# First branch of a hybrid layer: each direction's weights applied apart, with the tokens on the partitions

## The chip, the core and the metric

One NeuronCore of a Trainium2 chip runs the whole program. The metric is the device time of one execution in microseconds, the lower the better. The engines are TensorE (PE; PEld are its weight loads), VectorE (DVE), ScalarE (ACT), GpSimd (POOL), and SyncE (SP), which only issues transfers here.

## What is computed

Two "hybrid" layers (context of 256 and latent of 256 tokens, 1,024 channels) are followed by a second block of two layers. All of it is fp32. The change lies in the hybrid layers' first branch, a gated linear attention (mLSTM) with 4 heads (query and key 128 wide, value 256), run over the tokens forwards and backwards:

```
a   = exp(dmat - m_row) * (q k^T)            # per direction; dmat masks keys behind or ahead
den = sum_s(a)
h   = (a @ v) / max(|den|, exp(-m_row))      # per direction
y_a = rmsnorm(h_fwd + h_bwd) * a_norm_w * sigmoid(o) * silu(z)      # norm over a head's 256 channels
y   = sigmoid(mg_a) * (y_a @ w_a_out) + sigmoid(mg_b) * ... + sigmoid(mg_c) * ...
```

The reference does this in chunks with a carried state. The kernel computes the masked 512 x 512 weights of each head in closed form. In layer 1 only the 256 latent tokens are queries; keys and values are all 512.

## The kernel before

Each engine runs a program written out by hand, one Python function per engine (`tensor_program`, `scalar_program`, `vector_program`, `pool_program`, `sync_program`), and each of them calls `branch_a(l)`, `merge(l, "a")`, `branch_b(l)` and so on, in this order. The order of the work is the order of the calls. Between engines a `wait_ge` waits for a named event of another engine (`("a_av", l, h, c)` is the value product of layer l, head h, half c). Nothing is planned at run time.

**Weights.** `plan_units` lists the weight matrices in units of 2,048 words per partition, in the order of use. SyncE loads a unit into one of two `raw` buffers. `convert(u)` splits it: ScalarE rounds it to fp32r (`wh`, L1306 and L1307), VectorE subtracts to get the rest (`wl`, L1837 and L1839). `used(tag, j)` stands in both programs where a unit has been used up, and converts the unit two further on. A projection is three fp32r matmuls per 128 input channels (`mm3`, through `mm` at L483): `proj_t` gives channels on the partitions, tokens in the columns; `proj_k` gives tokens on the partitions (the values).

**The head loop of the first branch.** Everything of a token lies in four tiles of 128; layer 1 uses tiles 2 and 3 as queries. In TensorE's `branch_a`, for head h:

1. "pick": two 4-row matmuls broadcast the head's row of log weights to banks 2 and 3. ScalarE's exponentials and VectorE's `a_diag` (with the masks) turn it into `a_f` and `a_b`, one [key, query] matrix per direction.
2. Scores: four matmuls into banks 4 to 7, keys on the partitions, queries in the columns. VectorE multiplies them into `a_f` and `a_b` (`a_at`).
3. Projections o and z (banks 0 and 1, two halves each); ScalarE applies sigmoid and silu.
4. Denominators: `a_f` and `a_b` times a column of ones (one-column matmuls into bank 2); VectorE forms the reciprocal in four small operations; eight matmuls spread it over all partitions (`a_rd`).
5. VectorE multiplies the spread reciprocals into `a_f` and `a_b`; GpSimd adds the two (`a_mix`). TensorE meanwhile projects q and k of head h + 1.
6. Value product (`a_av`): value stationary, mixed weights moving, output channels on the partitions, into banks 4 and 5. It waits for GpSimd.
7. Between the two halves of the value projection of head h + 1, the sums of squares over the 256 channels are taken by one-column matmuls (`sums`); VectorE's `root` finds the inverse square root in 12 small operations; after the second half, `spread` broadcasts it, ScalarE copies it out (`a_rr`), VectorE multiplies it in (`a_y`), and GpSimd applies the gate.
8. ScalarE writes the rounded result to `YB[0]`, GpSimd the rest to `YB[1]`: the merge's operand.

The next head's pick waits for `a_mix`, its scores for `a_y` and `a_rr`. After head 3 there are no projections of a next head; steps 4 to 7 run alone, and then `merge` starts with two gate projections. The matmuls of steps 2, 4, 6 and 7 are plain fp32 and show as two records each. The two memsets of `a_f` and `a_b`, once a layer, and the products in steps 5, 7 and 8 are GpSimd's `branch_a`.

A helper records each operation, so one line stands for many: L483 is any matmul, L487 any transpose, L1296 any activation, L1818, L1822, L1823, L1826 and L1829 are VectorE's `tt`, `ts`, `stt` and `cp`, L2547 is GpSimd's `tt`. Groups are told apart by their tiles: TM is the scratch area that holds all `a_` tiles, colS the small columns, PS the PSUM banks, T the constant tables.

Of the kernel before, what the change touches and what calls it, by code (L numbers as in the profile page):

```python
# [198 lines left out]
def program(nc, wpk, xin, memt, vec, tabs, tabs2, rpb, out):  # L199
# [10 lines left out]
    with ctx:  # L210
# [123 lines left out]
        def lay(l):  # L334
# [11 lines left out]
        a_fg = [a_hs[p, 0] for p in dirs]  # L346
        a_zero = [a_hs[p, 1] for p in dirs]
# [7 lines left out]
                   {0: ((256, 512),), 1: ((0, 128), (256, 512)), 2: (), 3: ((256, 384),)})  # L355

# [122 lines left out]
        def tensor_program(P):  # L479
# [53 lines left out]
            def ada_unit(q):  # L533
# [48 lines left out]
            def branch_a(l):  # L582
# [2354 lines left out]
```

## Time and profile before

| | |
|---|---|
| median of 3 runs | 2703.24 us (2700.78 to 2704.4) |
| the profiled execution | 2704.5 us, its span 2702.7 us |
| TensorE busy | 2452.9 us (91%), 16,496 records |
| VectorE busy | 1322.9 us (49%) |
| ScalarE busy | 1030.7 us (38%) |
| GpSimd busy | 335.9 us (12%) |
| transfers | 291.48 MB, mean 108 GB/s |

The span is the stretch from the first to the last instruction, and the execution's time has a little around it. A busy TensorE isn't one at its peak, since the ends of matmuls are modelled: the distance between the starts of two of them is the better measure. Its clock is granted at one of two levels, 1.2 and 2.4 GHz; PEclk in a stretch is the mean as a share of the upper one.

### The profile page before, as it was taken

How to read it: one execution, taken by the hardware profiler on the slowest of the kernel's cores; microseconds unless marked ns; L12 is line 12 of the kernel's file. 1: busy time of each engine (PE TensorE's matmuls, PEld its weight loads, DVE VectorE, ACT ScalarE, POOL GpSimd, SP SyncE). 2: the span in 40 equal slices, each digit the busy share in tenths (PEclk: the TensorE clock that was granted, in tenths of full speed). 3: DMA queues.
4: the chain of work that ended last, by engine and by line, in shares of the span. 5: the costliest groups of instructions: out<-in, count | busy, mean ns of one | idle time of the engine just before them, and what ended most of it. 6: DMA issues, size and time to landing. Idle time of an engine off the chain costs nothing.

```text
span 2702.7 us, 38973 instructions
## 1 busy us (share of the span) xinstructions
PE 2452.9 (91%) x16496; PEld 2196.6 (81%) x16496; DVE 1322.9 (49%) x2682; ACT 1030.7 (38%) x1893; POOL 335.9 (12%) x340
## 2 busy tenths in 40 slices
PE   6999989999988999779889999997898999888998
PEld 3777767988867988668889888897767999867998
DVE  4433322577633223553345665345655555656554
ACT  2333311344431222243333444444354444444443
POOL 1011110222201021011112230110100010100010
PEclk9899989999999999889889999998898999988999
DMA  5211114211123212132223223444213445302444
GB/s 231 94 55 55 63 63 167 99 63 63 56 101 140 94 52 104 55 99 77 78 94 141 79 79 125 141 173 141 94 63 109 163 171 191 130 19 105 172 168 144
DMA packets 50413, 291.48 MB, mean 108 GB/s; under 512 B 8960, under 2 KB 13312, under 8 KB 19072
## 3 DMA queue, kind: packets, MB, share of 16 engines
q1 hardware_dynamic: 50240, 289.00, 30.1%
q8 instruction: 129, 2.11, 0.3%
q14 instruction: 44, 0.36, 0.0%
HBM read 286.89 MB, written 2.36 MB: 107 GB/s over the span
## 4 chain that ended last, share of the span: by engine, by line
PE 72%; DVE 14%; ACT 5%; DMA 3%; issue 1%; SPq 1%; POOL 1%; DVEq 0%; ACTq 0%; POOLq 0%
PE PS L483 70%; DVE wl L1837 3%; DMA raw<-in_wpk 3%; ACT wh L1306 2%; DVE wl L1839 2%; PE PS L487 2%; DVE TM L1818 1%; ACT TM L1296 1%; ACT TMG L1296 1%; DVE colS L1826 1%; DVE HYl L1826 1%; DVE TMG L1826 1%; POOL TM L2547 1%; ACT HYh L1296 1%; DVE TM L1826 1%
## 5 line engine op out<-in xcount | busy, mean ns | idle before, releaser
L483 PE MATMUL PS<-HYh,wh 128*128 128x256 f32 (+1 forms) x3000 | 966.2, 322 | 58.2 <-DVE HYl L1826 30.5
L483 PE MATMUL PS<-HYl,wh 128*128 128x256 f32 (+1 forms) x3000 | 948.8, 316 | 0.0
L483 PE MATMUL PS<-HYh,wl 128*128 128x256 f32 (+1 forms) x3000 | 948.0, 316 | 0.0
L1837 DVE TENSOR_TENSOR wl<-raw,wh 128x1280 fp32r<-128x1280 f32 (+2 forms) x254 | 368.6, 1451 | 720.8 <-ACT wh L1306 720.8
L483 PEld LDWEIGHTS PS<-HYh,wh 128*128 128x128 f32 x3000 | 590.9, 197 | 105.1 <-DVE HYl L1826 35.5
L483 PEld LDWEIGHTS PS<-HYl,wh 128*128 128x128 f32 x3000 | 591.0, 197 | 29.5
L483 PEld LDWEIGHTS PS<-HYh,wl 128*128 128x128 f32 x3000 | 589.0, 196 | 31.7
L1306 ACT ACTIVATE wh<-raw 128x1280 fp32r<-128x1280 f32 (+2 forms) x254 | 306.6, 1207 | 386.0 <-PE PS L483 246.8
L1296 ACT ACTIVATE TM<-PS 128x512 f32<-128x512 f32 (+4 forms) x363 | 175.4, 497 | 720.0 <-PE PS L483 590.6
L483 PE MATMUL PS<-wh,HYh 128*128 128x256 f32 x1458 | 424.5, 291 | 13.0 <-DVE HYl L1826 11.2
L483 PE MATMUL PS<-wl,HYh 128*128 128x256 f32 x1458 | 414.5, 284 | 0.0
L483 PE MATMUL PS<-wh,HYl 128*128 128x256 f32 x1458 | 414.5, 284 | 0.0
L483 PEld LDWEIGHTS PS<-wh,HYh 128*128 128x128 f32 x1458 | 281.4, 193 | 17.9 <-DVE HYl L1826 12.0
L483 PEld LDWEIGHTS PS<-wl,HYh 128*128 128x128 f32 x1458 | 281.4, 193 | 0.3
L483 PEld LDWEIGHTS PS<-wh,HYl 128*128 128x128 f32 x1458 | 281.2, 193 | 0.1
L483 PE MATMUL PS<-TM 128*128 128x128 f32 (+5 forms) x848 | 215.1, 440 | 60.8 <-DVE TM L1826 22.7
L1839 DVE TENSOR_TENSOR wl<-raw,wh 128x768 fp32r<-128x768 f32 (+2 forms) x254 | 248.1, 977 | 0.0
L483 PEld LDWEIGHTS PS<-TM 128*128 128x128 f32 (+2 forms) x848 | 130.7, 210 | 105.8 <-DVE TM L1826 26.4
L1307 ACT ACTIVATE wh<-raw 128x768 fp32r<-128x768 f32 (+2 forms) x254 | 206.7, 814 | 0.0
L2547 POOL TENSOR_TENSOR TM<-TM 128x512 f32<-128x512 f32 (+1 forms) x96 | 95.3, 1003 | 568.9 <-DVE TM L1818 205.6
L2547 POOL TENSOR_TENSOR HYl<-TM,HYh 128x256 fp32r<-128x256 f32 (+2 forms) x68 | 74.6, 1098 | 689.9 <-ACT HYh L1296 689.9
L1296 ACT ACTIVATE TMG<-PS 128x512 f32<-128x512 f32 (+2 forms) x122 | 54.1, 443 | 161.1 <-PE PS L483 147.1
(176 smaller groups left out, 1955.3 us busy)
## 6 DMA issues: line engine op xcount, KB each, us to landing
raw<-in_wpk SPq DMA_DIRECT2D x235, 1024.0 KB, 4.8
raw<-in_wpk SPq DMA_DIRECT2D x32, 704.0 KB, 4.1
TM<-in_wpk SPq DMA_DIRECT2D x4, 1024.0 KB, 18.2
X<-in_xin SPq DMA_DIRECT2D x1, 2048.0 KB, 9.8
Y<-in_wpk SPq DMA_DIRECT2D x2, 1024.0 KB, 23.9
Y<-bias_d SPq DMA_DIRECT2D x4, 512.0 KB, 10.2
raw<-in_wpk SPq DMA_DIRECT2D x3, 512.0 KB, 3.7
T<-in_tabs SPq DMA_DIRECT2D x1, 1216.0 KB, 14.7
```

Of the source, the lines that this page charges most:

```text
L483: return P.x.matmul(o, l, r, start=start, stop=stop)
L487: return P.x.transpose(o, i, ident[0:p, 0:p])
L1296: return A.x.activation(o, i, f, **kw).then_inc(*act_step.mark(*events))
L1306: A.x.activation(wh[:, s, 0:c], raw[:, r, 0:c], ACT.Copy).then_inc(*hi_split.mark((u, 0)))
L1307: A.x.activation(wh[:, s, c:n], raw[:, r, c:n], ACT.Copy).then_inc(*hi_split.mark((u, 1)))
L1818: return D.x.tensor_tensor(o, a, b, op).then_inc(*dve_step.mark(*events))
L1826: return D.x.scalar_tensor_tensor(out=o, in0=a, scalar=s, in1=b, op0=op0, op1=op1).then_inc(*dve_step.mark(*events))
L1837: D.x.tensor_tensor(wl[:, s, 0:c], raw[:, r, 0:c], wh[:, s, 0:c], ALU.subtract).then_inc(*lo_split.mark())
L1839: D.x.tensor_tensor(wl[:, s, c:n], raw[:, r, c:n], wh[:, s, c:n], ALU.subtract).then_inc(*lo_split.mark(u))
L2547: return G.x.tensor_tensor(o, a, b, op).then_inc(*pool_step.mark(*events))
```

## The change

The directions are no longer mixed before the value product. TensorE multiplies each direction's weights, stationary and still not normalised, with the values as the moving side: the output has the tokens on the partitions and 256 channels in the columns (`a_banks`: two banks for a token tile, one per direction). The values have a 257th column of ones, so the last output column is the denominator. Key tiles that are masked out wholly are left out (`a_keys`, `a_valid`). Per token tile VectorE takes the two denominators (four small operations), ScalarE copies direction 0 times its reciprocal (`a_hf`), VectorE adds direction 1 times its own (`a_h`), and ScalarE squares with a sum over the channels. One `root` gives the norm per token, ScalarE scales (`a_hn`), TensorE transposes 128 x 128 blocks back (`outputs_turned`), between the two value halves of the next head, or between the first two gate projections of the merge. VectorE multiplies with the norm weight and the gate, ScalarE writes the rounded half, VectorE the rest (`outputs`, `outputs_high`). With three token tiles' banks in PSUM, tile 3 of layer 0 waits for the first tile's `a_h`. Sigmoid and silu become tanh of half the argument; the factors of two are taken into VectorE's products and the norm. GpSimd has no work left in the branch. Events that others wait for are renamed to match.

```diff
-a_qk, a_v, a_f, a_b = tm(0, [2, 512]), tm(1024, [4, 256]), tm(2048, [4, 512]), tm(4096, [4, 512])
+a_qk, a_v, a_f, a_b = tm(0, [2, 512]), tm(1024, [4, 257]), tm(2052, [4, 512]), tm(4100, [4, 512])
 a_dirs = (a_f, a_b)
-a_g, a_hs, a_rr, a_gt = tm(6144, [2, 512]), tm(8192, [2, 512]), tm(9216, [2, 512]), TMG[:, 0:512]
+a_g, a_z, a_h, a_rr = tm(6148, [2, 512]), tm(7172, [2, 512]), tm(8196, [4, 256]), tm(8196, [2, 512])
+a_gt, a_junk = TMG[:, 0:512], TMG[:, 512:768]
...
+a_valid = ({0: ((0, 512),), 1: ((128, 512),), 2: ((256, 512),), 3: ((384, 512),)},
+           {0: ((0, 128), (256, 512)), 1: ((0, 512),), 2: ((256, 384),), 3: ((256, 512),)})
+a_keys = ([[0], [0, 1], [0, 1, 2], [0, 1, 2, 3]], [[0, 1], [1], [0, 1, 2, 3], [0, 1, 3]])
+def a_banks(l, i):
+    b = 2 + 2 * ((i - 2 * l) % 3)
+    return PS[:, b:b + 2]

...
-                P.wait_ge(act_step, ("a_z", l, h - 1, 0))
+                P.wait_ge(dve_step, ("a_z", l, h - 1, 0))
...
-                P.wait_ge(dve_step, ("a_mix", l, h - 1))
+                P.wait_ge(dve_step, ("a_h", l, h - 1, 3))
...
-                P.wait_ge(dve_step, ("a_y", l, h - 1))
-                P.wait_ge(act_step, ("a_rr", l, h - 1))
+                P.wait_ge(dve_step, ("a_y", l, h - 1, 1))
...
             P.wait_ge(act_step, ("a_exp", l, h))
-            for d in range(2):
-                for i in range(i0, 4):
-                    js = [[j for j in range(4) if j <= i], [0, 1, 2, 3][i:2] if i < 2 else [0, 1] + [2, 3][i - 2:]][d]
-                    for n_, j in enumerate(js):
-                        t = mm(bank(2)[:, 4 * d + i:4 * d + i + 1], a_dirs[d][:, j, 128 * i:128 * i + 128], one[:, 0:1],
-                               n_ == 0, n_ == len(js) - 1)
-            t.then_inc(*pe_step.mark(("a_den", l, h)))
-            P.wait_ge(dve_step, ("a_rd", l, h))
-            for d in range(2):
-                for i in range(i0, 4):
-                    c = 8 + 4 * d + i
-                    t = mm(bank(2 + d)[:, 128 * i:128 * i + 128], colS[:, c:c + 1].to_broadcast([128, 128]), ident)
-            t.then_inc(*pe_step.mark(("a_rd", l, h)))
+            P.wait_ge(act_step, ("a_v", l, h, 1))
+            for i in range(i0, 4):
+                if i - i0 == 3:
+                    P.wait_ge(dve_step, ("a_h", l, h, i0))
+                for d in range(2):
+                    js = a_keys[d][i]
+                    for j in js:
+                        t = mm(a_banks(l, i)[:, d, 0:257], a_dirs[d][:, j, 128 * i:128 * i + 128], a_v[:, j], j == js[0], j == js[-1])
+                t.then_inc(*pe_step.mark(("a_out", l, h, i)))
             if h < 3:
                 qk_unit(h + 1)
-            P.wait_ge(pool_step, ("a_mix", l, h))
-            P.wait_ge(act_step, ("a_v", l, h, 1))
-            for c in range(2):
-                for j in range(4):
-                    lo = a_lo(j, t0)
-                    t = mm(bank(4 + c)[:, lo:512], a_v[:, j, 128 * c:128 * c + 128], a_f[:, j, lo:512], j == 0, j == 3)
-                t.then_inc(*pe_step.mark(("a_av", l, h, c)))
-            if h < 3:
                 v_half(h + 1, 0)
-            P.wait_ge(act_step, ("a_sq", l, h))
-            sums(6, [a_hs[:, 0, 0:N], a_hs[:, 1, 0:N]], N, o256[:, 0:1], 1, 0, ("a_sums", l, h))
-            if h < 3:
+                outputs_turned(l, h)
                 v_half(h + 1, 1)
-            P.wait_ge(dve_step, ("a_root", l, h))
-            spread(6, colS[:, 24:28], N, 1, 0, ("a_spread", l, h))
+    def outputs_turned(l, h):
+        i0 = 2 * l
+        P.wait_ge(act_step, ("a_hn", l, h))
+        for c in range(2):
+            for i in range(i0, 4):
+                t = turned(bank(4 + c)[:, 128 * (i - i0):128 * (i - i0) + 128], a_h[:, i, 128 * c:128 * c + 128])
+            t.then_inc(*pe_step.mark(("a_yt", l, h, c)))
...
                 gate(u, 0, 0)
+                if br == "a":
+                    outputs_turned(l, 3)
                 gate(u, 128, 1)
...
-                    A.wait_ge(pool_step, ("a_y", l, h - 1, 1))
-                act(a_g[:, c, 0:N], bank(c)[:, 0:N], ACT.Sigmoid, ("a_o", l, h, c))
+                    A.wait_ge(dve_step, ("a_y", l, h - 1, 1))
+                act(a_g[:, c, 0:N], bank(c)[:, 0:N], ACT.Tanh, ("a_o", l, h, c), scale=0.5)
             used("a_o", 4 * l + h)
             for c in range(2):
                 A.wait_ge(projected, ("a_z", l, h, c))
                 if h:
-                    A.wait_ge(pool_step, ("YB", l, "a", 2 * h - 2))
-                act(a_hs[:, c, 0:N], bank(c)[:, 0:N], ACT.Silu, ("a_z", l, h, c))
+                    A.wait_ge(dve_step, ("YB", l, "a", 2 * h - 2))
+                act(a_z[:, c, 0:N], bank(c)[:, 0:N], ACT.Tanh, ("a_zt", l, h, c), scale=0.5)
             used("a_z", 4 * l + h)
+            for i in range(t0 // 128, 4):
+                A.wait_ge(dve_step, ("a_rd", l, h, i))
+                if h:
+                    A.wait_ge(pe_step, ("a_yt", l, h - 1, 1))
+                act(a_h[:, i], a_banks(l, i)[:, 0, 0:256], ACT.Copy, ("a_hf", l, h, i), scale=colS[:, 8 + 2 * i:9 + 2 * i])
+                A.wait_ge(dve_step, ("a_h", l, h, i))
+                A.wait_own(act_step)
+                act(a_junk, a_h[:, i], ACT.Square, ("a_sq", l, h), scale=0.5, accum_out=colS[:, 24 + i:25 + i])
+            A.wait_ge(dve_step, ("a_root", l, h))
+            for i in range(t0 // 128, 4):
+                act(a_h[:, i], a_h[:, i], ACT.Copy, ("a_hn", l, h), scale=colS[:, 28 + i:29 + i])
             if h < 3:
-                A.wait_ge(pe_step, ("a_s", l, h, 3))
                 qk(h + 1)
-            for c in range(2):
-                A.wait_ge(pe_step, ("a_av", l, h, c))
-                A.wait_ge(pool_step, ("a_gate", l, h))
-                act(a_hs[:, c, 0:N], bank(4 + c)[:, t0:512], ACT.Square, ("a_sq", l, h))
-            if h < 3:
                 v_half(h + 1, 0)
+                outputs_high(l, h)
                 v_half(h + 1, 1)
-            A.wait_ge(pe_step, ("a_spread", l, h))
-            act(a_rr[:, 0, 0:N], bank(6)[:, 0:N], ACT.Copy, ("a_rr", l, h))
-            A.wait_ge(pool_step, ("a_y", l, h, 1))
-            if h == 0 and l:
-                A.wait_ge(projected, ("m_value", 0, "c", 7))
-            act(YB[0][:, 2 * h:2 * h + 2, t0:512], a_hs[:, :, 0:N], ACT.Copy, ("YB", l, "a", 2 * h))
+    def outputs_high(l, h):
+        t0, N = lay(l)
+        A.wait_ge(dve_step, ("a_y", l, h, 1))
+        if h == 0 and l:
+            A.wait_ge(projected, ("m_value", 0, "c", 7))
+        act(YB[0][:, 2 * h:2 * h + 2, t0:512], a_z[:, :, 0:N], ACT.Copy, ("YB", l, "a", 2 * h))
...
-            act(TMG[:, 512 * (j % 3):512 * (j % 3) + N], bank(j % 2)[:, 0:N], ACT.Sigmoid, ("m_gate", l, br, j))
+            f, x = (ACT.Tanh, 0.5) if br == "a" else (ACT.Sigmoid, 1.0)
+            act(TMG[:, 512 * (j % 3):512 * (j % 3) + N], bank(j % 2)[:, 0:N], f, ("m_gate", l, br, j), scale=x)
...
                 gate(0)
+                if br == "a":
+                    outputs_high(l, 3)
                 gate(1)
...
+        D.x.memset(a_v[:, :, 256:257], 1.0).then_inc(*dve_step.mark())
         for h in range(4):
             if h:
-                D.wait_ge(pe_step, ("a_av", l, h - 1, 1))
-                D.wait_ge(pool_step, ("a_mix", l, h - 1))
-                for j, a in ((1, 0), (3, 256)):
-                    if a >= t0:
-                        D.x.memset(a_f[:, j, a:a + 128], 0.0).then_inc(*dve_step.mark(("a_zero", l, h)))
-            else:
-                D.wait_ge(pool_step, ("a_zero", l))
+                D.wait_ge(pe_step, ("a_out", l, h - 1, 3))
             D.wait_ge(pe_step, ("a_pick", l, h))
             for d in range(2):
                 for j in range(i0, 4):
...
             for j in range(4):
                 D.wait_ge(pe_step, ("a_s", l, h, j))
-                lo = a_lo(j, t0)
                 for d in range(2):
-                    if ("a_ex", l, h, d, j) in act_step.at:
-                        D.wait_ge(act_step, ("a_ex", l, h, d, j))
-                    D.wait_own(dve_step) if j == 0 and d == 0 else None
-                    tt(a_dirs[d][:, j, lo:512], bank(4 + j)[:, lo:512], a_dirs[d][:, j, lo:512], ALU.mult, ("a_at", l, h))
+                    for a, z in a_valid[d][j]:
+                        a = max(a, t0)
+                        if z > a:
+                            D.wait_ge(act_step, ("a_ex", l, h, d, j))
+                            tt(a_dirs[d][:, j, a:z], bank(4 + j)[:, a:z], a_dirs[d][:, j, a:z], ALU.mult, ("a_at", l, h))
             used("a_o", 4 * l + h)
+            for c in range(2):
+                D.wait_ge(act_step, ("a_zt", l, h, c))
+                stt(a_z[:, c, 0:N], a_z[:, c, 0:N], 1.0, bank(c)[:, 0:N], ALU.add, ALU.mult, ("a_z", l, h, c))
+            D.wait_own(dve_step)
+            stt(a_g[:, :, 0:N], a_g[:, :, 0:N], 1.0, a_z[:, :, 0:N], ALU.add, ALU.mult)
             used("a_z", 4 * l + h)
-            D.wait_ge(pe_step, ("a_den", l, h))
...
-            for j in range(4):
-                lo = a_lo(j, t0)
-                tt(a_f[:, j, lo:512], a_f[:, j, lo:512], bank(2)[:, lo:512], ALU.mult)
-                tt(a_b[:, j, lo:512], a_b[:, j, lo:512], bank(3)[:, lo:512], ALU.mult, ("a_mixed", l, h, j), ("a_mix", l, h))
+            for i in range(i0, 4):
+                den = colS[:, 8 + 2 * i:10 + 2 * i]
+                D.wait_ge(pe_step, ("a_out", l, h, i))
+                cp(den, a_banks(l, i)[:, :, 256])
+                D.wait_own(dve_step)
+                stt(den, den, -1.0, den, ALU.mult, ALU.max)
+                D.wait_own(dve_step)
+                tt(den, den, a_cm.rearrange("p (d i) h -> p d i h", d=2)[:, :, i, h], ALU.max)
+                D.wait_own(dve_step)
+                D.x.reciprocal(den, den).then_inc(*dve_step.mark(("a_rd", l, h, i)))
+                D.wait_ge(act_step, ("a_hf", l, h, i))
+                D.wait_own(dve_step)
+                stt(a_h[:, i], a_banks(l, i)[:, 1, 0:256], den[:, 1:2], a_h[:, i], ALU.mult, ALU.add, ("a_h", l, h, i))
+            D.wait_ge(act_step, ("a_sq", l, h))
+            root(colS[:, 28 + i0:32], colS[:, 20 + i0:24], colS[:, 24 + i0:28], ("a_root", l, h), eps=64 * EPS)
             if h < 3:
                 used("a_qk", 4 * l + h + 1)
-            D.wait_ge(pe_step, ("a_sums", l, h))
-            root(colS[:, 24:24 + N // 128], colS[:, 28:28 + N // 128], bank(6)[:, 0:N // 128], ("a_root", l, h))
-            if h < 3:
+                outputs(l, h)
                 used("a_v", 4 * l + h + 1)
-            D.wait_ge(act_step, ("a_rr", l, h))
-            for c in range(2):
-                stt(a_hs[:, c, 0:N], bank(4 + c)[:, t0:512], vcol(f"anw{l}", 2 * h + c), a_rr[:, 0, 0:N], ALU.mult, ALU.mult,
-                    ("a_y", l, h), ("a_y", l, h, c))
+    def outputs(l, h):
+        t0, N = lay(l)
+        for c in range(2):
+            D.wait_ge(pe_step, ("a_yt", l, h, c))
+            stt(a_z[:, c, 0:N], bank(4 + c)[:, 0:N], vcol(f"anw{l}", 2 * h + c), a_g[:, c, 0:N], ALU.mult, ALU.mult, ("a_y", l, h, c))
+        D.wait_ge(act_step, ("YB", l, "a", 2 * h))
+        D.wait_own(dve_step)
+        tt(YB[1][:, 2 * h:2 * h + 2, t0:512], a_z[:, :, 0:N], YB[0][:, 2 * h:2 * h + 2, t0:512], ALU.subtract,
+           ("YB", l, "a", 2 * h), ("YB", l, "a", 2 * h + 1))
...
-                tt(Y[:, j, t0:512], bank(2 + j % 2)[:, 0:N], sg, ALU.mult, ("m_value", l, br, j))
+                stt(Y[:, j, t0:512], sg, 1.0, bank(2 + j % 2)[:, 0:N], ALU.add, ALU.mult, ("m_value", l, br, j))
...
+        if br == "a":
+            outputs(l, 3)
```

## Rows read from the trace of the kernel before

**Rows 1.** The page, part 4: the chain that ended last, shares of the span by engine.

```profile
PE 72%; DVE 14%; ACT 5%; DMA 3%; issue 1%; SPq 1%; POOL 1%; DVEq 0%; ACTq 0%; POOLq 0%
```

**Rows 2.** Busy time by stretch: us, engines, PEclk (granted clock), DMA.

```profile
core 0: us, PE busy (x) PEld busy (x) DVE busy (x) ACT busy (x) POOL busy (x), PEclk, DMA share, GB/s
...
122.50:369.40 246.90, 224.04 (x1142) 185.82 (x1140) 79.02 (x182) 72.62 (x119) 39.28 (x32) 0.88 0.15 52
...
1210.40:1390.00 179.60, 154.39 (x1014) 144.35 (x1014) 65.81 (x167) 61.77 (x104) 24.46 (x32) 0.88 0.23 82
...
337.60:369.40 31.80, 22.48 (x98) 17.89 (x96) 8.84 (x26) 3.68 (x5) 5.12 (x5) 0.64 0.00 1
...
511.80:512.60 0.80, 0.80 (x10) 0.80 (x9) 0.80 (x2) 0.25 (x1) 0.00 (x0) 1.00 0.00 0
```

**Rows 3.** TensorE's timeline, layer 0, head 1: start us, us, instruction, idle before.

```profile
195.38 4.52 PE L483 MATMUL PS<-T,TM 128*128 128x1 f32 x40
...
204.23 0.77 PE L483 MATMUL PS<-HYh,wh 128*128 128x512 f32 x1
...
216.39 5.32 PE L483 MATMUL PS<-TM 128*128 128x512 f32 x16
...
221.36 0.47 PE L483 MATMUL PS<-wh,HYh 128*128 128x256 f32 x1
...
227.29 1.84 PE L483 MATMUL PS<-T,TM 128*128 128x1 f32 x16
...
234.84 1.05 PE L483 MATMUL PS<-T,colS 128*128 128x128 f32 x8
...
240.56 4.54 PE L483 MATMUL PS<-TM 128*128 128x512 f32 x8 [3.61 <-DVE TM L1826]
...
244.75 0.58 PE L483 MATMUL PS<-HYh,wh 128*128 128x512 f32 x1
...
266.73 4.52 PE L483 MATMUL PS<-T,TM 128*128 128x1 f32 x40
```

**Rows 4.** Waits of TensorE from 122.5 to 369.4 us: total us, times, longest.

```profile
PE PS L483 <- DVE TM L1826: 10.8, 3, 3.6
```

**Rows 5.** VectorE's timeline, layer 0, head 1: conversion; first and last of 12 root operations.

```profile
197.37 1.50 DVE L1837 TENSOR_TENSOR wl<-raw,wh 128x1280 fp32r<-128x1280 f32 x1 [8.52 <-ACT wh L1306]
...
229.17 0.16 DVE L1822 TENSOR_SCALAR small<-PS 128x4 f32<-128x4 f32 x1 [8.43 <-PE PS L483]
...
231.35 0.16 DVE L1826 SCALAR_TENSOR_TENSOR colS<-colS 128x4 f32<-128x4 f32 x1
```

**Rows 6.** Groups of instructions by form, ScalarE and VectorE, whole span.

```profile
L1296 ACT ACTIVATE TM<-PS,colS 128x256 f32<-128x256 f32 x22 | 10.0, 470 | 21.0 <-DVE colS L1822 10.9 <-PE PS L483 10.1
...
L1826 DVE SCALAR_TENSOR_TENSOR X<-PS,ada,X 128x256 f32<-128x256 f32 x24 | 10.9, 480 | 26.7 <-PE PS L483 26.7
```

**Rows 7.** TensorE's timeline, second branch, layer 0: eight transposes.

```profile
511.71 1.04 PE L487 MATMUL PS<-T,TM 128*128 128x128 f32 x8
```

**Rows 8.** TensorE's timeline, layer 1, heads 1 to 3 and the merge's first matmul.

```profile
1262.91 3.18 PE L483 MATMUL PS<-T,TM 128*128 128x1 f32 x28
...
1269.11 0.56 PE L483 MATMUL PS<-HYh,wh 128*128 128x256 f32 x1
...
1299.68 3.78 PE L483 MATMUL PS<-TM 128*128 128x256 f32 x8 [3.95 <-DVE TM L1826]
...
1302.90 0.77 PE L483 MATMUL PS<-HYh,wh 128*128 128x256 f32 x1
...
1315.89 3.18 PE L483 MATMUL PS<-T,TM 128*128 128x1 f32 x28
...
1368.63 3.18 PE L483 MATMUL PS<-T,TM 128*128 128x1 f32 x28
...
1390.03 0.56 PE L483 MATMUL PS<-HYh,wh 128*128 128x256 f32 x1
```

**Rows 9.** Groups of ScalarE between 60 and 1480 us: activation table loads.

```profile
L1296 ACT ACT_TABLE_LOAD x33 | 42.3, 1283 | 0.6
```

More of the change, by code:

```diff
@@ L338, in program @@
         GROUPS = ((0, 0), (1, 256))
-        a_qk, a_v, a_f, a_b = tm(0, [2, 512]), tm(1024, [4, 256]), tm(2048, [4, 512]), tm(4096, [4, 512])
+        a_qk, a_v, a_f, a_b = tm(0, [2, 512]), tm(1024, [4, 257]), tm(2052, [4, 512]), tm(4100, [4, 512])
         a_dirs = (a_f, a_b)
-        a_g, a_hs, a_rr, a_gt = tm(6144, [2, 512]), tm(8192, [2, 512]), tm(9216, [2, 512]), TMG[:, 0:512]
+        a_g, a_z, a_h, a_rr = tm(6148, [2, 512]), tm(7172, [2, 512]), tm(8196, [4, 256]), tm(8196, [2, 512])
+        a_gt, a_junk = TMG[:, 0:512], TMG[:, 512:768]
         dirs = (slice(0, 4), slice(32, 36))
         a_i = [a_gt[p] for p in dirs]
-        a_fg = [a_hs[p, 0] for p in dirs]
-        a_zero = [a_hs[p, 1] for p in dirs]
+        a_fg = [a_z[p, 0] for p in dirs]
+        a_zero = [a_z[p, 1] for p in dirs]
         a_r = [rows[p] for p in dirs]
@@ L702, in value @@
                         P.wait_ge(dve_step, ("c_uc", l, 3, 1))
-                    proj_t(bank(2 + j % 2)[:, 0:N], u, c, 128, YB, lambda k: (pool_step, ("YB", l, br, k)), 0, 8, t0, N,
+                    proj_t(bank(2 + j % 2)[:, 0:N], u, c, 128, YB, lambda k: ((dve_step if br == "a" else pool_step), ("YB", l, br, k)), 0, 8, t0, N,
                            ("m_value", l, br, j), *([("unit", u)] if c else []))
@@ L814, in branch_b @@
                 t0, N = lay(l)
-                free[6] = (dve_step, ("ada", 14)) if l == 0 else (act_step, ("a_rr", l, 3))
-                free[7] = (dve_step, ("ada_row", 15)) if l == 0 else (act_step, ("a_rr", l, 3))
+                free[6] = (dve_step, ("ada", 14)) if l == 0 else (dve_step, ("a_h", l, 3, 3))
+                free[7] = (dve_step, ("ada_row", 15)) if l == 0 else (dve_step, ("a_h", l, 3, 3))
                 P.wait_ge(rest_in, "all")
-                P.wait_ge(dve_step, ("a_y", l, 3))
+                P.wait_ge(dve_step, ("a_y", l, 3, 1))
                 P.wait_ge(*free[6])
@@ L1341, in v_half @@
                     if h:
[L1342 to L1343 removed]
+                        A.wait_ge(pe_step, ("a_out", l, h - 1, 3))
+                    act(a_v[:, 2 * b:2 * b + 2, 0:256], v2(b), ACT.Copy, ("a_v", l, h, b))
                     if b:
@@ L1842, in used, with root @@
                 convert(unit_after(place[tag, j]))
-            def root(y, t, ss, *events, square=None, times=None, more=None):
+            def root(y, t, ss, *events, square=None, times=None, more=None, eps=EPS):
                 n = y.shape[1]
@@ L1851, in root @@
                 elif square is None:
-                    ts(v, ss, EPS, None, ALU.add, None, *[("in", e) for e in events])
+                    ts(v, ss, eps, None, ALU.add, None, *[("in", e) for e in events])
                 else:
@@ L1988, in branch_a @@
-                    used("a_o", 4 * l + h)
-                    used("a_z", 4 * l + h)
-                    D.wait_ge(pe_step, ("a_den", l, h))
-                    dc = colS[:, 8:16].rearrange("p (d i) -> p d i", d=2)[:, :, i0:4]
-                    dn = colS[:, 16:24].rearrange("p (d i) -> p d i", d=2)[:, :, i0:4]
-                    pd = bank(2)[:, 0:8].rearrange("p (d i) -> p d i", d=2)[:, :, i0:4]
-                    cp(dn, pd)
-                    D.wait_own(dve_step)
-                    stt(dc, dn, -1.0, dn, ALU.mult, ALU.max)
@@ L2547, in tt @@
                 return G.x.tensor_tensor(o, a, b, op).then_inc(*pool_step.mark(*events))
-            def branch_a(l):
-                t0, N = lay(l)
-                G.wait_ge(dve_step, ("a_rc", l))
-                G.wait_ge(act_step, ("a_ln", l))
-                G.x.memset(a_f[:], 0.0).then_inc(*pool_step.mark())
-                G.x.memset(a_b[:], 0.0).then_inc(*pool_step.mark(("a_zero", l)))
-                for h in range(4):
-                    for c in range(2):
-                        G.wait_ge(act_step, ("a_z", l, h, c))
-                        tt(a_g[:, c, 0:N], a_g[:, c, 0:N], a_hs[:, c, 0:N], ALU.mult, ("a_gate", l, h))
-                    for j in range(4):
-                        lo = a_lo(j, t0)
-                        G.wait_ge(dve_step, ("a_mixed", l, h, j))
-                        tt(a_f[:, j, lo:512], a_f[:, j, lo:512], a_b[:, j, lo:512], ALU.add, ("a_mix", l, h))
-                    for c in range(2):
-                        G.wait_ge(dve_step, ("a_y", l, h, c))
-                        G.wait_own(pool_step)
-                        tt(a_hs[:, c, 0:N], a_hs[:, c, 0:N], a_g[:, c, 0:N], ALU.mult, ("a_y", l, h, c))
-                    G.wait_ge(act_step, ("YB", l, "a", 2 * h))
-                    G.wait_own(pool_step)
-                    tt(YB[1][:, 2 * h:2 * h + 2, t0:512], a_hs[:, :, 0:N], YB[0][:, 2 * h:2 * h + 2, t0:512], ALU.subtract,
-                       ("YB", l, "a", 2 * h), ("YB", l, "a", 2 * h + 1))
             def merge(l, br):
```

27 lines of the change are left out of this document (8 added, 19 removed).

## Prediction

> **What bounds the kernel now.** I began with the chain of waits: TensorE holds 72% of it, VectorE 14%, and nothing else over 5% [rows 1]. A change pays what it takes from TensorE's own stream: matmuls, waits, or time at the lower clock. The stage view then prices the first branch in both layers, from the end of head 0's z projection to the merge's first matmul: 246.9 us in layer 0, 179.6 us in layer 1, at a mean granted clock of 0.88, so some of it at the lower of the two levels (1.2 instead of 2.4 GHz) [rows 2]. TensorE's timeline for one head of layer 0 shows why. Between the z projection's end (195.38) and the next one's (266.73) lie 71.35 us. The projections in it are needed anyway; the rest is: denominators by one-column matmuls and their spread over the partitions until 204.23; the value matmuls from 216.39 to 221.36; norm sums (227.29) and norm spread (234.84); and 3.61 us idle, released by VectorE's normalised output, ahead of the scores at 240.56 [rows 3]. The waits view gives that idle three times, 10.8 us [rows 4]. So the bound here is TensorE's order of work with its hand-overs. VectorE, ScalarE and GpSimd matter where TensorE waits for them.
>
> **Layer 0, heads 0 to 2, piece by piece** [rows 3].
> - Denominators and spread, 195.38 to 204.23, 8.85 us, go. In their place stand 20 matmuls of 257 columns (3, 3, 7, 7 for the four token tiles: one per direction and key tile that is not masked out). Nearest row: the old value matmuls, 3,072 columns in 221.36 - 216.39 = 4.97 us, 0.0016 us a column, so 0.41 us each and 8.2 us in all.
> - A new wait: the fourth tile reuses the first one's banks and waits for its sum h. Count from the z projection's end. VectorE converts weights from 2.0 us on (197.37 - 195.38) [rows 5], for 2.3 us. Ahead of it now stand the z products and the 1,024-wide gate product. By size they lie between 0.48 us for 256 columns [rows 6] and 1.49 for 1,280 [rows 5]: 0.7 for 512, 1.2 for 1,024. They push the conversion's end from 4.3 to about 5.0. Then follows a link per tile: four small operations at 0.2 us (the root's step: 12 in 2.34 us [rows 5]), ScalarE's scaled copy 0.47, VectorE's multiply-add 0.48 [rows 6], and 0.2 for three hand-overs: 1.95. The first h is ready at 6.95. TensorE has done 13 of 20 matmuls at 5.3, waits 1.6, and ends at 9.9. The block costs 1.05 more than the old one.
> - The query and key projections took 12.16 (204.23 to 216.39) for 48 records; the o and z projections took 21.98 for 96 at full clock, so 48 cost 11.0. The excess is the clock, which had fallen over the one-column matmuls. Dense work precedes them now: -1.2. The bound is that nothing of this comes back.
> - The value matmuls (4.97) go, inside the count above.
> - Norm sums (227.29 to the next projection, 1.7) become 8 transposes, 1.04 [rows 7]: -0.7. Norm spread, from 234.84 to the row broadcasts (1.1 us long, then the idle): -1.0.
> - The 3.61 us idle goes. What is late next? The scores wait for the outputs' last multiplication (bank 4). It follows the transposes, which stand ahead of the second half of the value projection (5.84 us, 227.29 + 1.7 to 234.84); two multiplications of about 0.7 us fit. The tile links end at 12.8, square with its accumulator read 0.6, root 2.3, four scaled copies 1.9: the transposes can go at 17.6, while TensorE gets there near 27. In front of them ScalarE copies q late, at about 18, needed at 20.9.
>
> Sum: +1.05 - 1.2 - 5.0 - 0.7 - 1.0 - 3.6 = -10.4, a period of 60.9. Three old periods are 246.9 - 31.8 = 215.1 [rows 2]; 3 x 60.9 = 182.7: **-32.4 us**.
>
> **Layer 0, head 3** has nothing to hide behind: 31.8 us from 337.6 to 369.4 [rows 2]. Now the merge's first gate projection (5.5) goes ahead of the transposes: TensorE has them at 15.4, waits until 17.6, ends at 18.6; less the gate work done meanwhile, 13.1: **-18.7**. The merge's first value projection needs the two last output tiles. Two multiplications, ScalarE's copy (1.1) and VectorE's subtraction (1.2, moved from GpSimd) end near 22.2; the second gate projection covers until 24.
>
> **Layer 1** has half the queries [rows 8]. Period 52.98 (1262.91 to 1315.89). Denominators and spread 6.20 become 14 x 0.41 = 5.8 with no reused bank: -0.4. Query and key projections -1.1 for the clock. Value matmuls (2,048 columns at 0.0016) -3.3. Sums and norm spread become 4 transposes: -0.9. The idle -3.95. The scores, 3.22 from 1299.68 to 1302.90, are 1,024 columns, 1.65 at the upper level: -1.6. Output and z projections 12.99 against 11.7 at full clock: -1.3. That is -12.5, or 40.5. ScalarE now has the exponentials less far ahead of the o copy, so I add 0.4 for a wait: 40.9. (179.6 - 21.4) - 3 x 40.9 = **-35.5**. Last head: h at 4.2 + 2 x 1.95 = 8.1, square, root and two copies 11.95, transposes 12.45, less 2.9 of gate work, 9.5 instead of 21.40: **-11.9**.
>
> **Costed at nothing.** The table loads: 33 from before the branch of layer 0 to after that of layer 1, at 1.28 us [rows 9]; exp, sigmoid and silu alternate, three loads a head. With tanh in their place they fall away on ScalarE, which waits for TensorE at those places. If tanh and exp don't share a table, 1.3 us land before layer 1's output gates, some 5 us in all. GpSimd's work in the branch goes, its memsets, products and mixing sums. VectorE drops eight mixing multiplications and part of the masking ones, and gains three gate products, four multiply-adds, twelve small operations and the subtraction: at the sizes above some 3 us more a head, where it is busy 79.0 of 246.9 us [rows 2]; its cover is TensorE's projections, and without it the 3 us a head would show, 24 in all. Weight loads keep their order. No DMA is added or moved.
>
> Together 51.1 + 47.4 = 98.5 us. The profiled execution took 2704.5 (span 2702.7), 1.3 above the median of the runs; against the median I forecast **2605 us**.
>
> **A rule weighed.** A stretch with 8 fp32 transposes between projections was granted the full clock, 1.00, and they took 1.04 us, 0.13 each [rows 2, 7]. The Trainium skill, "TensorE: Matmul & The Clock Gate", Part 4, PE-mode transpose, says some 275 ns for one in context, and that transposing doesn't count as activity for the clock. By that page 48 transposes would cost 13 us instead of 6, and the sum would be about 91; the trace has a duration, so it decides.
>
> **Rivals.**
> - *Hand-overs bound* (0.12). The tile link crosses VectorE and ScalarE twice; no row shows that ping-pong. Bounds: 1.45 with hand-overs that cost nothing and 0.3 less of small operations; above, doubled to 3.9. Then in layer 0 the first h comes at 8.9 and q's copy at 25.7 against 22.7: 4.9 a head, 7.6 in the last; in layer 1 2.0 a head and 3.9 in the last: 14.7 + 7.6 + 6 + 3.9 = 32, time 2637. Against it: VectorE's small operations follow each other at 0.2 without a gap [rows 5].
> - *The new matmuls are dearer* (0.12). Their stationary side changes each time, and 257 columns is an odd row. The one-column matmuls price a weight load alone: 4.52 us for 20, 0.23 each [rows 3]. If none hides, 4 x 20 + 4 x 14 = 136 times 0.23 is 31: 2636. Against: the old value matmuls hid theirs.
> - *Tables stay* (0.06): 2610, above.
> - *Slower, by the clock* (0.03). Place: from the transposes on. If fp32 outputs and transposes leave the clock at the lower level, then what follows in a head (second value half, pick, scores, o and z: 33 us in layer 0, 20 in layer 1) runs at half rate: 3 x 33 + 3 x 20 = 159 more, 2764. It decides once more than 98 us of full-rate work is slowed. For it: 0.64 was granted in the last head, with its idle and one-column work [rows 2]. Against: fp32 work with columns kept its rate (4.97), and the transposes' 1.00. The page named above points this way; by its sentence on transposes alone this rival would hold.
> - *Half done* (0.03): a new wait that I haven't seen costs over 35 us. That is not slower.
>
> **Numbers.** The forecast has 0.64, its own range 2596 (no wait for the reused bank, 4 x 1.6, and by estimate 2 us of clock regained in the merges' first gates) to 2618 (half of the 15.6 us of clock not regained, and 5 of tables). The range 2596 to 2637 takes in tables and dearer matmuls, and the edge of the hand-overs. A difference within 0.2%, 5.4 us, can't be told from none; no case falls there but the tail of the clock's. Faster 0.96, same 0.01, slower 0.03.
>
> **What would show it.** Right: no one-column matmuls in the first branch; 40 records of 257 columns in about 8.2 us plus one wait near 1.6 for VectorE; periods near 61 and 41; no idle before the scores; one table load between the first exponential of the branch and the third branch. Clock of the two stretches above 0.95. Wrong: idle ahead of value projections, released by ScalarE (hand-overs); record spacing above 0.21 (dearer); a clock under 0.9 in periods without idle.

## The result, and the profile after

| | before | changed |
|---|---|---|
| median | 2702.01 us (4 runs, 2698.1 to 2704.4) | 2591.84 us (4 runs, 2589.59 to 2595.54) |
| the profiled execution, its span | 2704.5 us, 2702.7 us | 2593.25 us, 2591.4 us |

The ratio is 0.9595, with a 95% interval of 0.9578 to 0.9612: 110 us faster. The forecast was 2605, its range 2596 to 2637. The direction was right, and so was most of the gain; the gain was larger than forecast by 12 us, and the time lies 4 us below the range, so the forecast missed.

The page of the changed kernel, parts 1 and 4:

```profile
PE 2381.4 (92%) x16176; PEld 2138.1 (83%) x16176; DVE 1338.5 (52%) x2735; ACT 1018.7 (39%) x1939; POOL 257.1 (10%) x264
...
PE 75%; DVE 14%; ACT 5%; DMA 2%; issue 1%; SPq 1%; POOL 1%; DVEq 0%; ACTq 0%; POOLq 0%
```

TensorE holds a little more of a shorter chain than in [rows 1]. The stages of [rows 2], from the end of head 0's z projection to the transposes of the merge (columns as there):

```profile
121.80:316.00 194.20, 189.20 (x974) 159.14 (x973) 89.64 (x226) 77.51 (x164) 0.00 (x0) 1.00 0.19 66
1146.80:1280.90 134.10, 131.25 (x911) 123.01 (x909) 68.28 (x171) 57.72 (x117) 0.00 (x0) 1.00 0.30 110
```

Read the third value from the end, the granted clock: 1.00 in both stretches, rounded (the one dip is named below), where it was 0.88 in both. GpSimd has nothing left, VectorE has 10.6 us more work in layer 0 and TensorE doesn't wait for it beyond the waits below. The waits of TensorE in these two windows, all there are, against 10.8 us for one of its kinds alone in [rows 4]:

```profile
PE PS L492 <- DVE TM L1835: 3.9, 4, 1.0
PE PS L496 <- ACT TM L1298: 1.1, 1, 1.1
...
PE PS L496 <- ACT TM L1298: 2.8, 1, 2.8
```

The 2.8 us (2.85 in the timeline) are the wait of layer 1's last head for its scaled tiles. It is too close to the window's end to show in the mean, but the four transposes behind it ran at the lower level, and so did the next 2.4 us of the merge's second gate projection:

```profile
1280.07:1280.83 0.76, 0.76 (x4) 0.76 (x5) 0.04 (x1) 0.21 (x1) 0.00 (x0) 0.50 0.00 0
```

TensorE's timeline for layer 0, head 1, from one z projection's end to the next (the second row is cut off by the end of the view's window: seven matmuls stand there):

```profile
180.69 5.81 PE L492 MATMUL PS<-TM 128*128 128x257 f32 x26
187.48 0.70 PE L492 MATMUL PS<-TM 128*128 128x257 f32 x2 [0.98 <-DVE TM L1835]
...
190.43 0.58 PE L492 MATMUL PS<-HYh,wh 128*128 128x512 f32 x1
...
201.53 0.28 PE L492 MATMUL PS<-wh,HYh 128*128 128x256 f32 x1
...
207.28 1.04 PE L496 MATMUL PS<-T,TM 128*128 128x128 f32 x8
...
214.00 1.13 PE L492 MATMUL PS<-rows,T 4*128 4x512 f32 x4
215.05 2.85 PE L492 MATMUL PS<-TM 128*128 128x512 f32 x8
217.55 0.58 PE L492 MATMUL PS<-HYh,wh 128*128 128x512 f32 x1
...
239.55 5.81 PE L492 MATMUL PS<-TM 128*128 128x257 f32 x26
```

The period is 58.86 us against 71.35. The output matmuls stand at the head, 26 records (13 matmuls) in 5.81 us, 0.45 each with the end of the last one; then one wait of 0.98 for the first tile's sum; no idle ahead of the scores (215.05), and they take 2.50 us until the o projection starts (217.55), where they took 4.19 before.

That last number is the one that the prediction had wrong. The stages view of just these scores, before and after, says what differs:

```profile
240.56:244.75 4.19, 4.19 (x8) 2.05 (x9) 2.18 (x10) 2.10 (x2) 2.88 (x3) 0.59 0.56 231
```

```profile
215.05:217.55 2.50, 2.50 (x10) 1.46 (x9) 1.66 (x2) 1.54 (x2) 0.00 (x0) 1.00 0.00 0
```

The same eight records ran at a mean granted clock of 0.59 before, behind the idle 3.61 us, and at 1.00 after: mostly at the lower of the engine's two levels, 1.2 GHz, then, and wholly at the upper, 2.4 GHz, now.

### The profile page after: what moved, and what is told of

Its sections match the earlier page's. It is cut to its first block, busy times and chain, and to the rows that moved or that the text cites. A ratio compares the mean times of both kernels' runs of the same rounds, so it can differ in the third digit from the quotient of the medians.

```text
span 2591.4 us, 38368 instructions
## 1 busy us (share of the span) xinstructions
PE 2381.4 (92%) x16176; PEld 2138.1 (83%) x16176; DVE 1338.5 (52%) x2735; ACT 1018.7 (39%) x1939; POOL 257.1 (10%) x264
## 4 chain that ended last, share of the span: by engine, by line
PE 75%; DVE 14%; ACT 5%; DMA 2%; issue 1%; SPq 1%; POOL 1%; DVEq 0%; ACTq 0%; POOLq 0%
PE PS L492 73%; DVE wl L1846 3%; DVE wl L1848 2%; PE PS L496 2%; ACT wh L1308 2%; DMA raw<-in_wpk 2%; DVE TM L1827 2%; ACT TM L1298 1%; ACT TMG L1298 1%; DVE colS L1835 1%; DVE HYl L1835 1%; DVE TMG L1835 1%; DVE TM L1835 1%; ACT HYh L1298 1%; DVE colS L2287 1%
## 5 line engine op out<-in xcount | busy, mean ns | idle before, releaser
L1298 ACT ACTIVATE TM<-PS 128x512 f32<-128x512 f32 (+4 forms) x339 | 163.4, 497 | 566.7 <-PE PS L492 436.1
L492 PE MATMUL PS<-TM 128*128 128x128 f32 (+6 forms) x992 | 222.6, 404 | 32.0 <-ACT colC L1298 12.2
L492 PEld LDWEIGHTS PS<-TM 128*128 128x128 f32 (+2 forms) x992 | 148.3, 197 | 67.4 <-ACT colC L1298 13.4
L2561 POOL TENSOR_TENSOR HYl<-TM,HYh 128x256 fp32r<-128x256 f32 (+2 forms) x60 | 59.9, 1000 | 682.5 <-ACT HYh L1298 682.5
L1298 ACT ACTIVATE TMG<-PS,colS 128x512 f32<-128x512 f32 (+1 forms) x104 | 62.0, 602 | 82.8 <-DVE colS L1831 82.5
```

What stands on the lines that cost most here:

```text
L492: return P.x.matmul(o, l, r, start=start, stop=stop)
L1298: return A.x.activation(o, i, f, **kw).then_inc(*act_step.mark(*events))
L2561: return G.x.tensor_tensor(o, a, b, op).then_inc(*pool_step.mark(*events))
```

## The experiments

**Does a stretch that wasn't touched repeat?** From the second branch of layer 0 to the pick of layer 1's first head the two traces differ by 2.7 us. The kernel before, unchanged, was traced again.

> The kernel before, unchanged, for a second trace. The changed kernel's trace is 2.7 us shorter in the stretch between the two first branches (711.5 against 708.8 us from the second branch of layer 0 to the scores of layer 1's first head), which the change doesn't touch. Theory: that is scatter of single executions, and this trace differs from the first one by 1 to 4 us there, either way. Rival: the stretch repeats within 0.5 us, and the 2.7 us is an effect of the change. The head periods of layer 0 should repeat within 0.5 us (72.9, 71.35, 70.9) under both, unless the clock's share of them varies.

Ratio to the kernel before 0.9998 (0.9984 to 1.0012). Its span was 2695.2 us, 7.5 shorter than the first trace's. The stretch took 708.7 us, against 711.1 in the first trace and 708.4 in the changed kernel's. Over all traces of this study it lies between 708.3 and 711.1. So this is scatter, as is the wait ahead of layer 1's first scores (8.8 to 10.6 us over the traces). Two of layer 0's three periods repeated, 71.4 and 71.0; the first, 71.3, is 1.6 shorter than in the first trace, more than the 0.5 expected: in that one the denominators ran longer at the lower clock, the case that the expectation left open.

**What were the table loads worth, before and after?**

```diff
-act(a_g[:, c, 0:N], bank(c)[:, 0:N], ACT.Sigmoid, ("a_o", l, h, c))
+act(a_g[:, c, 0:N], bank(c)[:, 0:N], ACT.Tanh, ("a_o", l, h, c), scale=0.5)
...
-act(a_hs[:, c, 0:N], bank(c)[:, 0:N], ACT.Silu, ("a_z", l, h, c))
+act(a_hs[:, c, 0:N], bank(c)[:, 0:N], ACT.Tanh, ("a_z", l, h, c), scale=0.5)
```

(and likewise for the gates of this branch's merge)

> The kernel before with tanh in place of sigmoid and silu in the first branch and in its merge, and nothing else (the gates are another function of the projections). 26 of the 41 table loads should go. Theory (the loads lie beside TensorE's work): within 2 us of the kernel before. Rival (loads on the path): up to 26 x 1.28 = 33 us faster, and the gain that the prediction missed is part of it.

The trace has 15 table loads for the 41 of before. Ratio 1.0002 (0.9992 to 1.0012): nothing. The loads lay in ScalarE's slack. Then the same swap backwards, in the changed kernel, for all three activations:

```diff
-act(a_g[:, c, 0:N], bank(c)[:, 0:N], ACT.Tanh, ("a_o", l, h, c), scale=0.5)
+act(a_g[:, c, 0:N], bank(c)[:, 0:N], ACT.Sigmoid, ("a_o", l, h, c))
...
-act(a_z[:, c, 0:N], bank(c)[:, 0:N], ACT.Tanh, ("a_zt", l, h, c), scale=0.5)
+act(a_z[:, c, 0:N], bank(c)[:, 0:N], ACT.Silu, ("a_zt", l, h, c))
...
-f, x = (ACT.Tanh, 0.5) if br == "a" else (ACT.Sigmoid, 1.0)
+f, x = ACT.Sigmoid, 1.0
```

> The changed kernel with sigmoid and silu in place of tanh in the first branch and in its merge (the products with 1 + the gate stay, so the gates are another function). The table loads return, three a head. In the new order ScalarE has more to do between the z projection and the transposes, and the output gates of layer 1 follow the exponentials closely. Theory: layer 0 within 1 us; layer 1 0 to 1.3 us a head longer, 0 to 6 us in all. Rival (loads never matter): 0. Rival (loads in the tile chain of the last heads): both last heads 1.3 us longer and the others not.

Median 2608.14 us, ratio to the kernel before 0.9643 (0.9624 to 0.9662), where the changed kernel stands at 0.9595: about 13 us lost, where I had expected 0 to 6. Layer 0's periods are unchanged (58.86), and so is the time from the z projection to the transposes in the last heads (11.97 and 16.65 us), so the rival of the last heads is out. In heads 1 to 3 of layer 1 TensorE now waits ahead of the z projection, for the copy that frees its bank:

```profile
1178.83 0.39 PE L492 MATMUL PS<-HYh,wh 128*128 128x256 f32 x1 [2.41 <-ACT TM L1298]
```

ScalarE's timeline of this kernel shows two loads in a row with the exponentials between them:

```profile
1172.91 1.28 ACT L1298 ACT_TABLE_LOAD   x1 [2.26 <-DVE TM L1835]
1174.21 1.10 ACT L1298 ACTIVATE TM<-PS,colC 128x256 f32<-128x256 f32 x3
...
1177.10 1.28 ACT L1298 ACT_TABLE_LOAD   x1
1178.40 0.66 ACT L1298 ACTIVATE TM<-PS 128x256 f32<-128x256 f32 x2
```

Both of a head's loads lie on one chain, 2.57 us, and in two of the three heads the z projection behind the wait then took 7.4 and 7.3 us, at a granted clock of 0.77 and 0.78, for the 5.85 of the third. The three periods together are 10.9 us longer: 7.2 of waiting, 2.9 of clock, and the rest in the o projection. What is left up to 13 isn't shown by the one trace, whose span is 7.0 us longer. So the swap to tanh is worth nothing in the old order and some 11 to 13 us in the new one: with the idle time gone, ScalarE is close behind TensorE in layer 1.

**What does the place of the transposes hide, and does idle time cost its own length or more?**

```diff
-outputs_turned(l, h)
 v_half(h + 1, 1)
+outputs_turned(l, h)
```

(and likewise for `outputs_high` on ScalarE and for `outputs` with the conversion on VectorE)

> The changed kernel with the transposes after the second half of the next head's value projection, not before it, and the copies and conversions around them in the order of the kernel before. The outputs' multiplications then come after ScalarE's and VectorE's conversion, and the scores wait for them: by the rows of before, 3.7 us of idle time in each of six heads (the last heads are unchanged). Theory (the missed term is the clock after an idle stretch: the scores' 1,536 columns took 4.2 us after 3.6 us of waiting and 2.5 us in the changed kernel): the six scores' stretches grow by 1.5 us each beside the idle time, and the o projection after them by 0 to 0.6, so 31 to 36 us more in all, 2623 to 2628. Rival (the idle time alone): 22 us, 2614, with scores at 2.5 us.

Median 2626.23 us, 34.4 over the changed kernel (ratio to the kernel before 0.972, 0.9699 to 0.9741). The idle time is back, and the scores are slow again:

```profile
221.06 5.08 PE L492 MATMUL PS<-TM 128*128 128x512 f32 x8 [3.63 <-DVE TM L1835]
```

```profile
221.06:225.79 4.73, 4.73 (x8) 2.46 (x9) 3.30 (x9) 2.34 (x6) 0.00 (x0) 0.52 0.52 211
```

The three scores of layer 0 took 4.19, 4.73 and 4.76 us instead of 2.50, those of layer 1 3.05 to 3.22 instead of 1.64. The rival, the idle time alone, is 12 us short of what was measured. By the trace the six periods grew by 35.9 us: 22.8 of idle time, 10.8 in the scores, 1.9 in layer 1's o projections, and the rest in the transposes.

**The other way round: the kernel before, with its idle time filled.** This separates the clock from all else that changed.

```diff
 if h:
+    for _ in range(4):
+        mm(bank(7), ident, a_qk[:, 1])
     P.wait_ge(dve_step, ("a_y", l, h - 1))
```

> The kernel before with four matmuls more (128 x 512, fp32, 3.4 us at the upper clock, results unused, into bank 7) between the pick and the scores of heads 1 to 3, in both layers, where TensorE sat idle for 3.6 and 3.95 us. Nothing waits for less. Theory (the scores took 4.2 to 4.9 us instead of 2.5, and 3.2 instead of 1.6 in layer 1, because the idle time had brought the clock down): with the stretch filled the scores run at 2.5 and 1.6 us, and the kernel, with 24 matmuls more, is 9 to 13 us faster than the kernel before. Rival (the scores are slow for another reason, as the matmul's shape or the wait itself): no change, or slower by the 0 to 3 us by which the filling runs over.

Median 2691.09 us beside 2704.27 in the same session, ratio 0.9943 (0.9925 to 0.9961): 24 matmuls whose results nobody reads make the kernel 13 us faster. Its timeline and its stages view:

```profile
232.80 3.70 PE L483 MATMUL PS<-TM,T 128*128 128x512 f32 x8
236.49 2.85 PE L483 MATMUL PS<-TM 128*128 128x512 f32 x8
```

```profile
232.80:236.49 3.69, 3.69 (x11) 1.44 (x9) 3.69 (x5) 1.13 (x2) 0.64 (x1) 1.00 0.01 4
236.49:238.98 2.49, 2.49 (x9) 1.46 (x9) 2.17 (x10) 0.41 (x1) 1.91 (x2) 1.00 0.89 368
```

The filling takes the time of the old wait, the scores 2.49 us at clock 1.00. In layer 1 it takes 4.02 us, 0.32 of the wait is left, and the scores take 1.64. The six periods are 11.4 us shorter than in the second trace of the kernel before, 13.2 than in the first. The rival is out.

**What is the column of ones worth?**

```diff
 for j in js:
-    t = mm(a_banks(l, i)[:, d, 0:257], a_dirs[d][:, j, 128 * i:128 * i + 128], a_v[:, j], j == js[0], j == js[-1])
+    t = mm(a_banks(l, i)[:, d, 256:257], a_dirs[d][:, j, 128 * i:128 * i + 128], a_v[:, j, 256:257], j == js[0], j == js[-1])
...
+    t = mm(a_banks(l, i)[:, d, 0:256], a_dirs[d][:, j, 128 * i:128 * i + 128], a_v[:, j, 0:256], j == js[0], j == js[-1])
```

> The changed kernel without the 257th column in the output matmuls: per token tile the same stationary weights meet the column of ones in matmuls of their own, ahead of the 256-column ones. 80 + 56 = 136 one-column matmuls more, at 0.226 us each by the rows of before: 4.5 us a head in layer 0 (3.5 where the wait for the reused bank is covered) and 3.2 in layer 1. Theory: 27 to 31 us more, 2619 to 2623, with the query projection after them at full rate, because the 256-column matmuls stand between. Rival (one-column work draws the clock down, as in the kernel before, where q and k took 12.2 instead of 11.0 us): another 1 us or more a head, 2627 or more.

Median 2621.13 us, 29.3 over the changed kernel (ratio 0.9696, 0.9674 to 0.9717). Layer 0's output block grew from 9.74 to 12.93 us, layer 1's from 5.90 to 8.99. Over eight heads that is 25.1 us, and the two traces differ by 24.4; where the medians' other 4 us lie isn't shown. The stages view of the output block and of q and k:

```profile
182.71:195.64 12.93, 12.93 (x82) 11.88 (x80) 7.40 (x19) 5.43 (x12) 0.00 (x0) 1.00 0.24 82
195.64:206.72 11.08, 11.08 (x50) 9.17 (x49) 3.11 (x17) 3.17 (x8) 0.00 (x0) 1.00 0.00 0
```

One-column matmuls in groups of 3 and 7 between 256-column ones leave the clock at 1.00, while 40 records in a row, a wait and the spread had it at 0.75 in the kernel before, and q and k at 0.90. The wait isn't needed for that: in head 0 the clock fell among the one-column matmuls, before it:

```profile
125.00:128.80 3.80, 3.80 (x19) 3.80 (x18) 1.85 (x2) 0.18 (x1) 0.00 (x0) 0.50 0.15 39
```

**Can the waits that are left be had?** Two orders were tried apart and together: in layer 0 the conversion goes behind the tiles, and the last head's transposes go behind both gate projections.

```diff
-used("a_z", 4 * l + h)
+if l: used("a_z", 4 * l + h)
 for i in range(i0, 4):
...
+if l == 0: used("a_z", 4 * l + h)
```

(on ScalarE and on VectorE)

```diff
 gate(u, 0, 128)
-if br == "a": outputs_turned(l, 3)
 gate(u, 128, 1)
+if br == "a": outputs_turned(l, 3)
```

(and likewise for `outputs_high` on ScalarE)

> The changed kernel, layer 0 only: the weight conversion that stood between the z projection and the tile chain comes after the tiles (on ScalarE and VectorE both). The first tile's sum should then be ready 2.4 us earlier, and TensorE's wait of 0.98 us for the reused bank goes in four heads. Theory: 3.9 us faster than the changed kernel (2588), with head periods of 57.9 instead of 58.9 us, and the wait before the last head's transposes unchanged or shorter. Rival: the chain is held by TensorE's tiles and not by the conversion, and nothing changes; or the later conversion delays the value projection, and a wait of up to 1 us appears there.

> The changed kernel with the last head's transposes after both first gate projections of the merge, not between them. The waits of 1.09 us (layer 0) and 2.85 us (layer 1) ahead of the transposes should be covered. Theory: 3.5 us faster than the changed kernel, since the merge's first value projection needs the last two output tiles only after three quarters of its matmuls. Rival: the wait moves ahead of that projection's last matmuls, and the gain in layer 1 is 1 us or less.

> Both of the two changes just named: the late conversion in layer 0 and the transposes after both gate projections. Theory: they lie at different places and add up, 7.4 us faster than the changed kernel, 2584. Rival: the last head of layer 0 is bound by the same chain for both, and they add up to 6 us or less.

Medians 2588.05, 2588.79 and 2584.11 us (ratios 0.958, 0.9581 and 0.9562, each with about 0.002 on either side): 3.8, 3.1 and 7.7 us less than the changed kernel, as if they add. The first two are inside the intervals of the changed kernel's ratio, so here the traces decide, and not the medians. With the late conversion the output block takes 8.50 us in all four heads, not 9.74, and has no wait. With the transposes behind both gates, none of the waits of 1.09 and 2.85 is left, none appears in the value projections, and layer 1's transposes take 0.41 us instead of 0.77, at clock 1.00.

Last, the clock lesson put to use: the same version with unused matmuls in the wait ahead of each layer's first scores (with h == 0).

```diff
+for _ in range((3, 10)[l]):
+    mm(bank(4), ident, a_qk[:, 1])
 P.wait_ge(act_step, ("a_cm", l))
```

> The version with the late conversion and the transposes after both gate projections, and with unused matmuls in TensorE's wait ahead of the first head's scores: three in layer 0 (2.9 us idle) and ten in layer 1 (9 to 11 us idle). Theory: the first scores go from 4.9 (or 3.9) to 2.5 us in layer 0 and from 3.22 to 1.64 in layer 1, with up to 0.9 us more in layer 1's first output projection: 3 to 5 us faster, 2579 to 2581. Rival: the wait is set by transfers and conversions, which the filling doesn't touch, and the clock is already back: no change.

Median 2579.85 us, ratio 0.9534 (0.9518 to 0.9551). The version without it was measured in another session: the medians differ by 4.3 us, the ratios by 7.6, and their intervals overlap, so the size of this gain is open. What the trace shows is its place: the first scores took 2.50 us (4.93 without), layer 1's 1.64 (3.22). This is the fastest version here: 4.7% under the kernel before and 0.5 to 0.6% under the changed one.

## What the prediction had right, and which step failed

| term | forecast | measured |
|---|---|---|
| layer 0, three periods | -32.4 | -38.5 (3 x 58.86) |
| layer 0, last head | -18.7 | -19.9 |
| layer 1, three periods | -35.5 | -36.9 (3 x 40.42) |
| layer 1, last head | -11.9 | -11.5 |
| merges behind them | 0 | -1.8 |
| stretches not touched, scatter | 0 | -2.7 |

The two columns make -98.5 and -111.3, against the profiled executions' 111.25. The rows are differences of the two first traces; the stretches not named (the start, the passage between the layers, the end) are each within 1.7 us and cancel. That such a sum comes so near the medians' 110.2 is partly luck: the second trace of the kernel before was 7.5 us shorter than the first.

**The step that failed** is the last term of "Layer 0, heads 0 to 2": the idle time was to go at its own length, 3.61 us, and the scores behind it stood in the sum at what they had taken, 4.19 us. They had taken that at a clock of 0.59. In layer 1 the same piece was priced by its columns (-1.6); in layer 0 it was left out. By the 0.0016 us a column of the value matmuls, 1,536 columns are 2.5 us, and that is what the changed kernel shows: 2.50 at a clock of 1.00. In the forecast that is 1.7 us in each of three periods, 5.1 of the 6.1 us that the first row is off (most of the other 1.0 is the eight transposes, 0.79 us for the 1.04 of the forecast). With this term the forecast would have been 2600, and a range moved down by it would just have held the time. The experiments with the late transposes and with the filled idle time show the mechanism from both sides.

**Smaller ones.** In layer 1 0.4 us a head were added for a wait that didn't come, 1.2 of that row's 1.4. Layer 0's last head gained 1.2 more, by shorter tile links. The merges, forecast at no change (2 us were allowed for in the low end), ran 1.8 us faster: 0.6 is a shorter wait behind the first one, and in layer 1 the lower clock reached 4.5 us into the gates before and 2.4 us now. **The rest**, 2.7 us, is scatter of the first trace, as the second trace of the kernel before showed; the forecast had no width for it.

By its other steps:
- *Output matmuls*: 0.42 us each in layer 1 (14 in 5.90) and 0.43 in layer 0 where no wait divides them (20 in 8.50), for the forecast 0.41. At most 0.02 of a weight load's 0.23 shows; that rival is out.
- *The link of a tile*: 1.68 us (VectorE's multiply-adds at 186.94 and 188.62), forecast 1.95. The first sum came 6.7 us after the z projection, forecast 6.95, and TensorE waited 0.98, not 1.6, also because its 13 matmuls took 5.8. The rival of slow hand-overs is out:

```profile
186.94 0.48 DVE L1835 SCALAR_TENSOR_TENSOR TM<-PS,colS,TM 128x256 f32<-128x256 f32 x1 [0.54 <-ACT TM L1298]
...
188.62 0.48 DVE L1835 SCALAR_TENSOR_TENSOR TM<-PS,colS,TM 128x256 f32<-128x256 f32 x1 [0.54 <-ACT TM L1298]
```

- *Transposes*: 8 in 0.8 us from start to next start in heads 0 to 2 of layer 0, with the clock at 1.00 around them, as [rows 2] and [rows 7] said. The Trainium skill, "TensorE: Matmul & The Clock Gate", Part 4, PE-mode transpose, has some 275 ns for one, by estimate 2.2 us for eight, and says that they don't count as activity. These rows show neither 2.2 us nor a lower clock behind them. The slower rival is out: it needed the clock to stay low from the transposes on.
- *Last heads*: layer 1's transposes were ready 11.97 us after the z projection (forecast 11.95), layer 0's after 16.64 (forecast 17.6; four links of 1.68 instead of 1.95 make 1.1 of it).
- *Table loads at nothing*: right for what the change removes, by the first swap; and the changed kernel has one load, at 93.7 us, between the branch's first exponential and the third branch, as the prediction's signs asked. The price named for their staying, some 5 us in all, was too low: the second swap lost 11 to 13. I had put one load on layer 1's path, not the two that a head has there, and no clock.
- *Half of the clock's 15.6 us* was the upper bound of the time's own range. All that the clock had cost in these pieces came back, but that was less: the 15.6 is one head's rows taken three times, and over the six heads the same pieces had lost 11.8 us (layer 0's q and k 1.7; layer 1's q and k 4.0, scores 4.7, o and z 1.4). The error cancels, since the new periods were priced at full clock and set against the old ones as measured.

## What to carry to other kernels

Price each block that stands behind a wait at the full clock, by its columns, and not by its duration in the trace: when the wait goes, the slow start behind it goes too. Here six waits of 22.8 us in all had another 12.7 us of slow work behind them. A wait that can't be removed can be filled with matmuls nobody reads, if the bank is free and the filling fits in the wait. And before a step is called free because its engine has slack, ask whether the change itself uses up that slack: the same table loads cost nothing in the old order and 11 to 13 us in the new one.

## What I had not expected of the hardware

Filling 3.6 us of waiting brought scores from 4.2 to 4.9 us down to 2.49, and the whole kernel from 2704.3 to 2691.1 us with more work in it. Which waits lower the clock isn't settled by their length alone. Those of 0.98 and 1.09 us in the branch left it at 1.00. Those of 3.6 and 3.95 us lowered it each time. In between the same wait went both ways: 2.85 us ahead of layer 1's last transposes was followed by 0.50 in the changed kernel and by 1.00 in the run with the late transposes, and the 2.41 us of the swap backwards lowered it in two of three heads. I had taken the lower rate of the work behind a wait for that work's own.
